# A two-layer mixture block on one Trainium2 core: the experts' gate and up products with all eight K-tiles in three reduced-precision passes

## The reference

```python
D_MODEL = 1024; SEQ = 512; DEPTH = 2
N_GROUPS = 4; EXPERTS_PER_GROUP = 4; N_EXPERTS = 16; TOP_E = 2; EXPERT_FF = 256

def hier_moe(h, w_rg, b_rg, w_re, b_re, w_g, w_u, w_d):
    g_logits = (h @ w_rg + b_rg)                       # one of 4 groups for each token
    _, g_sel = lax.top_k(g_logits, 1)
    ...
    e_val, e_sel = lax.top_k(e_in_group, TOP_E)        # two of its 4 experts
    weights = jax.nn.softmax(e_val, axis=-1) * p_group
    gate = jnp.sum(one_hot(expert_id, N_EXPERTS) * weights[..., None], axis=2)
    hid = jax.nn.silu(jnp.einsum('bsd,edf->bsef', h, w_g)) * jnp.einsum('bsd,edf->bsef', h, w_u)
    hid = hid * gate[..., None]
    return jnp.einsum('bsef,efd->bsd', hid, w_d)
```

## Time and profile before

| what | value |
|---|---|
| median of three runs | 1389.27 us (1387.7 to 1389.38) |
| the profiled execution's own time | 1387.39 us |
| its span | 1385.6 us |
| PE busy | 1351.8 us, 98% |
| DVE, ACT, POOL busy | 892.1, 580.0, 761.6 us |
| expert loops | about 519 to 684 us and 1202 to 1373 us |

### The profile page before, as it was taken

How to read it: one execution, slowest core, us unless ns; L and a number is a source line. 1 busy time by engine, 2 the same in 40 slices (tenths; PEclk the granted TensorE clock), 3 DMA queues, 4 the chain that set the end, 5 groups by cost and what they waited for, 6 DMA issues and landing times.

```text
span 1385.6 us, 19946 instructions
## 1 busy us (share of the span) xinstructions
PE 1351.8 (98%) x6972; PEld 1046.3 (76%) x6972; DVE 892.1 (64%) x2057; ACT 580.0 (42%) x1238; POOL 761.6 (55%) x603
## 2 busy tenths in 40 slices
PE   7999999999999999999789999999999999999997
PEld 5788877777777876777577888777777778677774
DVE  4487866646684347988446787665566741588882
ACT  4323334343433135676343432434334321466761
POOL 4566654454345664567555576455444457546673
PEclk9999999999999999999989999999999999999999
DMA  5436422223222569999632242222223128699993
GB/s 155 131 93 175 128 71 87 62 78 105 84 67 67 203 269 349 354 371 369 135 116 76 61 137 78 79 77 72 83 90 90 62 76 291 238 368 365 357 345 87
DMA packets 115066, 225.35 MB, mean 163 GB/s; under 512 B 18666, under 2 KB 28324, under 8 KB 114958
## 3 DMA queue, kind: packets, MB, share of 16 engines
q1 hardware_dynamic: 102526, 198.64, 42.6%
q0 software_dynamic: 9936, 16.81, 5.3%
q10 hardware_dynamic: 2496, 8.52, 1.6%
HBM read 216.52 MB, written 31.25 MB: 179 GB/s over the span
## 4 chain that ended last, share of the span: by engine, by line
PE 92%; DVE 4%; POOL 1%; issue 1%; ACT 1%; DMA 1%; POOLq 0%; SPq 0%; DVEq 0%; ACTq 0%
PE bank L987 23%; PE bank L989 22%; PE bank L988 22%; PE bank L1284 5%; PE bank L1163 4%; PE bank L1175 3%; PE bank L1196 2%; PE bank L1244 2%; PE bank L1116 1%; PE bank L1186 1%; POOL w_lo L842 1%; PE bank L1129 1%; DVE probs L2003 1%; DVE mixed L1820 1%; PE bank L1254 1%
## 5 line engine op out<-in xcount | busy, mean ns | idle before, releaser
L836 POOL TENSOR_SCALAR w_hi<-raw 128x1024 fp32r<-128x1024 f32 (+2 forms) x142 | 149.8, 1055 | 409.3 <-PE bank L989 406.6
L842 POOL TENSOR_TENSOR w_lo<-raw,w_hi 128x512 fp32r<-128x512 f32 (+2 forms) x288 | 359.4, 1269 | 16.4 <-ACT w_hi L1732 4.6
L988 PE MATMUL bank<-w_hi,hT_lo 128*128 128x512 f32 (+2 forms) x696 | 258.7, 372 | 0.0
L987 PE MATMUL bank<-w_lo,hT_hi 128*128 128x512 f32 (+2 forms) x576 | 216.8, 376 | 2.0 <-DVE hT_lo L1828 1.0
L989 PE MATMUL bank<-w_hi,hT_hi 128*128 128x512 f32 (+2 forms) x576 | 211.7, 368 | 0.0
L987 PE MATMUL bank<-hT_lo,w_hi 128*128 128x512 f32 x384 | 159.4, 415 | 0.0
L989 PE MATMUL bank<-hT_hi,w_hi 128*128 128x512 f32 x384 | 150.7, 392 | 0.0
L988 PE MATMUL bank<-hT_hi,w_lo 128*128 128x512 f32 x384 | 150.2, 391 | 0.0
L988 PEld LDWEIGHTS bank<-w_hi,hT_lo 128*128 128x128 f32 x696 | 131.5, 189 | 20.2
L987 PEld LDWEIGHTS bank<-w_lo,hT_hi 128*128 128x128 f32 x576 | 108.7, 189 | 28.0 <-issue 8.5
L989 PEld LDWEIGHTS bank<-w_hi,hT_hi 128*128 128x128 f32 x576 | 108.6, 188 | 17.9
(11 more groups left out here) (359 smaller groups left out, 2836.5 us busy)
## 6 DMA issues: line engine op xcount, KB each, us to landing
raw<-in_w_gate SPq DMA_DIRECT2D x48, 512.0 KB, 3.8
work<-in_w_ff_gate SPq DMA_DIRECT2D x46, 512.0 KB, 6.5
work<-in_w_ff_up SPq DMA_DIRECT2D x46, 512.0 KB, 8.7
work<-in_w_ff_down SPq DMA_DIRECT2D x23, 1024.0 KB, 8.6
raw<-in_w_in SPq DMA_DIRECT2D x40, 512.0 KB, 3.6
raw<-in_w_branch SPq DMA_DIRECT2D x24, 512.0 KB, 3.6
w_lo_raw<-in_w_ff_down SPq DMA_DIRECT2D x10, 1024.0 KB, 8.1
X<-in_w_ff_gate SPq DMA_DIRECT2D x20, 512.0 KB, 5.8
```

The source lines that it names most:

```text
L836: nc.gpsimd.tensor_scalar(w_hi[:, two, :, 0:w], raw[:, slot, :, 0:w], 1.0, 0.0, ALU.mult, ALU.add).then_inc(split_hi, 1)
L842: last = nc.gpsimd.tensor_tensor(w_lo[:, two, kk, 0:w], raw[:, slot, kk, 0:w], w_hi[:, two, kk, 0:w].bitcast(F32), ALU.subtract)
L987: nc.tensor.matmul(out_ap, s_hi, m_lo, start=start, stop=False)
L988: nc.tensor.matmul(out_ap, s_lo, m_hi, start=False, stop=False)
```

## The change

`SPLIT_FROM` becomes 0: K-tiles 0 and 1 of experts 2 to 15 too are done in three passes. High and low parts of gate and up are made by whole pieces of four K-tiles (2048 elements a partition), two an expert, and the two pieces stand apart in the order of ACT and DVE. ACT takes over from DVE the right half of the rows (but expert 15's) and the hidden tile's high part. The overflow lists move from `e` 2 and 3 to 3 and 5, their product on PE from 5 to 7, and the wait for it from 6 to 8. The rest renames semaphores.

```diff
-FIRST_SPLIT, SPLIT_FROM = 2, 2
-SPLIT_PAIRS = (8 - SPLIT_FROM) // 2
+FIRST_SPLIT, SPLIT_FROM = 2, 0
...
-        gu_hi_bufs = [[oT_hi[:, 0:2], oT_hi[:, 2:4], oT_lo[:, 0:2], oT_lo[:, 2:4]],
-                      [hT_lo[:, 0:2], hT_lo[:, 2:4], hT_hi[:, 4:6], hT_hi[:, 6:8]]]
+        gu_hi_bufs = [[oT_hi[:, 0:4], oT_lo[:, 0:4]], [hT_lo[:, 0:4], hT_hi[:, 4:8]]]
...
-                    if e == 5:
+                    if e == 7:
                         pe.wait_ge(e_hot, 1)
...
-            def gate_up_hi(e):
-
-                for part, kk, kt in split_tiles():
-                    if kt == SPLIT_FROM or kk == 0:
-                        act.wait_ge(arrived(e, part), loaded(e, part))
-                    nc.scalar.activation(pair_hi_of(e, kt).rearrange("p k (h n) -> p k h n", h=2),
-                                         gate_up_piece(e, part)[:, :, kk:kk + 2, :].rearrange("p h k n -> p k h n"),
-                                         ACT.Copy).then_inc(gu_hi, 1)
+            def gate_up_hi(e, part):
+
+                first = 0 if part else SPLIT_FROM
+                act.wait_ge(arrived(e, part), loaded(e, part))
+                nc.scalar.activation(high_of(e, part), gate_up_piece(e, part)[:, :, first:4, :], ACT.Copy).then_inc(gu_hi, 1)
...
             def rows_down(e):
-                act.wait_ge(down_done, 2 * e + 1)
-                if e == 0:
-                    act.wait_ge(w_known, 1)
-                if e >= 4:
-                    act.wait_ge(y_out[l][e % 4], 16 * (e // 4))
-                nc.scalar.activation(xn[:, e % 4, 0:512], G[2][:, :], ACT.Copy,
-                                     scale=slot_weight[:, EXPERT_AT[e]:EXPERT_AT[e] + 1]).then_inc(y_act, 1)
-
+                for c in range(2 if e < N_EXPERTS - 1 else 1):
+                    act.wait_ge(down_done, 2 * e + c + 1)
+                    if e == 0 and c == 0:
+                        act.wait_ge(w_known, 1)
+                    if e >= 4 and c == 0:
+                        act.wait_ge(y_out[l][e % 4], 16 * (e // 4))
+                    nc.scalar.activation(xn[:, e % 4, c * 512:(c + 1) * 512], G[2 + c][:, :], ACT.Copy,
+                                         scale=slot_weight[:, EXPERT_AT[e]:EXPERT_AT[e] + 1]
+                                         ).then_inc((y_left, y_right)[c], 1)
+
+            def hidden_hi(e):
+                act.wait_ge(hid_turned, e + 1)
+                if e >= 2:
+                    act.wait_ge(down_done, 2 * (e - 1))
+                nc.scalar.activation(hid_hi[:, e % 2, :], T[e % 2][:, 0:FF], ACT.Copy).then_inc(hidT_hi, 1)
...
                     if e < N_EXPERTS - 1:
                         et_out(e + 1)
+                    if splits(e + 2):
+                        gate_up_hi(e + 2, 0)
+                    if 1 <= e < N_EXPERTS - 1:
+                        weights_hi(e)
                     if e >= 1:
                         rows_down(e - 1)
+                    if e < N_EXPERTS - 1:
+                        hidden_hi(e)
                     if e == N_EXPERTS - 1:
                         et_out(e + 1)
-                    if 1 <= e < N_EXPERTS - 1:
-                        weights_hi(e)
                     if splits(e + 2):
-                        gate_up_hi(e + 2)
+                        gate_up_hi(e + 2, 1)
...
+                    if splits(e + 1):
+                        gate_up_lo(e + 1, 1)
+                    if e == 0:
+                        hidden_lo(e)
+                        route_over()
+                    if splits(e + 2):
+                        gate_up_lo(e + 2, 0)
+                    if 1 <= e < N_EXPERTS - 1:
+                        down_lo_half(e)
...
+                    elif 1 <= e < N_EXPERTS:
+                        hidden_lo(e)
+                    if e == N_EXPERTS:
+                        rows_right(e - 1)
                     if e == 1:
                         route_rows()
-                    if splits(e + 2):
-                        gate_up_lo(e + 2)
-                    if e in (2, 3):
-                        route_blocks(e - 2)
-                    if e == 5:
+                    if e in (3, 5):
+                        route_blocks((3, 5).index(e))
+                    if e == 7:
```

More of the change, by code:

```diff
@@ L383, in first_native, with high_of @@
             return SPLIT_FROM if splits(e) else KT
-        def pair_hi_of(e, kt):
-            return gu_hi_bufs[e % 2][(kt - SPLIT_FROM) // 2]
+        def high_of(e, part):
+            first = 0 if part else SPLIT_FROM
+            return (gu_hi_bufs[e % 2][part].rearrange("p k n -> p (k n)")[:, 0:512 * (4 - first)]
+                    .rearrange("p (h k n) -> p h k n", h=2, n=FF))
         def tiles_of(slot_rows):
@@ L415, in in_runs @@
             return src.rearrange("a (j p k) n -> p (a j) (k n)", p=P, k=ROW_RUN)
-        def split_tiles():
-            return [(kt // 4, kt % 4, kt) for kt in range(SPLIT_FROM, KT, 2)]
         banks = [ctx.enter_context(nc.psum_tensor(f"bank{i}", [P, 512], F32)) for i in range(8)]
@@ L840, in split @@
                     if n == UNITS_K:
-                        pool.wait_ge(hi_by_act, kk + 1)
+                        pool.wait_ge(hi_by_left, kk + 1)
                     last = nc.gpsimd.tensor_tensor(w_lo[:, two, kk, 0:w], raw[:, slot, kk, 0:w],
@@ L903, in add_rows @@
                 def add_rows(e):
-                    pool.wait_ge(y_act, e + 1)
-                    pool.wait_ge(y_dve, e + 1)
+                    pool.wait_ge(y_left, e + 1)
+                    pool.wait_ge(y_right, e + 1)
                     if e == 0:
@@ L2271, in et_out, with gate_up_lo @@
                                         ALU.subtract).then_inc(et_dve, 1)
-            def gate_up_lo(e):
-                for n, (part, kk, kt) in enumerate(split_tiles()):
-                    v.wait_ge(gu_hi, split_pairs(e - 1) + n + 1)
-                    nc.vector.tensor_tensor(gate_up_low(e, part)[:, :, kk:kk + 2, :].rearrange("p h k n -> p k h n"),
-                                            gate_up_piece(e, part)[:, :, kk:kk + 2, :].rearrange("p h k n -> p k h n"),
-                                            pair_hi_of(e, kt).bitcast(F32).rearrange("p k (h n) -> p k h n", h=2),
-                                            ALU.subtract).then_inc(gu_lo, 1)
+            def gate_up_lo(e, part):
+                first = 0 if part else SPLIT_FROM
+                v.wait_ge(gu_hi, split_parts(e - 1) + part + 1)
+                nc.vector.tensor_tensor(gate_up_low(e, part)[:, :, first:4, :], gate_up_piece(e, part)[:, :, first:4, :],
+                                        high_of(e, part).bitcast(F32), ALU.subtract).then_inc(gu_lo, 1)
             def down_lo_half(e):
@@ L2286, in down_lo_half, with hidden_lo, rows_right @@
                                         w_hi[:, 1, :, :].bitcast(F32), ALU.subtract).then_inc(down_lo_dve, 1)
+            def hidden_lo(e):
+                v.wait_ge(hid_turned, e + 1)
+                v.wait_ge(hidT_hi, e + 1)
+                nc.vector.tensor_tensor(hid_lo[:, e % 2, :], T[e % 2][:, 0:FF], hid_hi[:, e % 2, :].bitcast(F32),
+                                        ALU.subtract).then_inc(hidT_done, 1)
+            def rows_right(e):
+                v.wait_ge(down_done, 2 * (e + 1))
+                if e >= 4:
+                    v.wait_ge(y_out[l][e % 4], 16 * (e // 4))
+                if e == 0:
+                    v.wait_ge(w_known, 1)
+                nc.vector.tensor_scalar(xn[:, e % 4, 512:1024], G[3][:, :], slot_weight[:, EXPERT_AT[e]:EXPERT_AT[e] + 1],
+                                        None, ALU.mult).then_inc(y_right, 1)
             def experts():
```

54 lines of the change are left out of this document (18 added, 36 removed).

## The result

| what | before | after |
|---|---|---|
| median beside each other | 1388.49 us (4 runs) | 1401.8 us (4 runs, 1401.23 to 1402.97) |
| ratio | | 1.0097, 95% interval 1.0082 to 1.0112 |
| profiled execution, its span | 1387.39, 1385.6 us | 1401.77, 1400.0 us |
| PE, DVE, ACT, POOL busy | 1351.8, 892.1, 580.0, 761.6 us | 1350.9, 927.0, 623.5, 811.9 us |

The kernel became 13.3 us slower. The direction is the forecast's (slower, at a chance of 0.53), the size is not: 5.5 us were forecast, and the result lies above the range's end of 1399.5.

The account below looks back on a forecast made before the run. PE, holding 92% of the span, was taken as the bound, with DVE, ACT and POOL close behind. -9.8 - 0.4 + 5.3 + 10.4 = +5.5 us on 1389.27 gave 1394.8 us, range 1384.5 to 1399.5.

Parts of the forecast that it names:

- PE's gain: Experts 2 to 15, both layers: 56 K-tiles in three passes instead of full float32 save 0.176 us each, -9.8 us.
- the tail: End of each layer: ScalarE takes the eviction before the last hidden tile's copy, 0.2 us a layer, -0.4 us.
- The entry: Start of the expert stage: PE waits 2.4 and 2.9 us before the weight counts, behind ACT's late hidden copy; +5.3 us.
- DVE's term: Experts: DVE's 7.4 us of work plus two 1.1 us handovers with POOL exceed PE's 9.38; 5.2 a layer, +10.4 us.
- it is a toss: After expert 7 DVE has caught up; one handover or two an expert is open, half counted, 0.8 us a layer.
- rival A: Experts: only one handover each, DVE needs 8.5 of 9.38 us; -2.9 us, 1386.4 us; chance 0.2.
- rival C: DVE is the bound in all experts, also after 7: 7.5 us a layer, +10.1, 1399.4 us; chance 0.1.
- 1.4 + 3.0: Per layer: DVE late by 0.23 us in each of experts 1 to 6, 1.4; overflow lists no longer absorbed, 3.0.
- The tie: Whether POOL asks before or after DVE's second piece begins; the walk had the two within 0.05 us.
- the held gather: POOL gather started 0.16 us after a DVE subtraction lasted 2.00 us; such holding could leave one handover.
- Rival B: One handover an expert, but late weight loads cost 1 to 1.5 us a layer: no change, 1389 us; chance 0.2.

Follow-up runs that it names:

- e8: e7 with a semaphore of its own for the second half of each expert's gate/up rows; 1378.95 us.
- e1: The changed kernel, but ACT copies expert 0's hidden high part ahead of expert 2's first high part instead of behind it; 1395.97 us.
- e2: The changed kernel, but DVE makes both halves of the down weights' low part from expert 1 on and POOL none; 1392.64 us.
- e14: The changed kernel with the edits of e1 and e8, POOL's two subtractions an expert kept; 1397.04 us.
- e13: e8, but POOL makes one 128x512 subtraction of the low down rows an expert, DVE the other and the right half; 1385.89 us.
- e7: The changed kernel with the edits of e1 and e2 together; 1382.34 us.
- e4: The changed kernel with the overflow lists back in experts 2 and 3 and PE's overflow counts two experts earlier; 1400.53 us.
- e5: The kernel before with all eight K-tiles in three passes, pairs and old order kept; 1398.75 us.
- e6: The changed kernel with two K-tiles left as before; new order, whole pieces, ACT's evictions and spread lists stay; 1394.25 us.
- e3: The changed kernel with POOL's subtraction for experts 1 to 14 left out and not replaced, so the output is not the block's; 1390.65 us.
- e12: e2 with three matmuls on ready data put before PE's weight counts in expert 1; 1387.91 us.

## Why the prediction was wrong in size

The forecast's sum, term by term, against the runs. They form a chain: before 1387.8, e8 1378.95, e1 1395.97, after 1401.8.

- **PE's gain**, -10.2 with the tail: e8, in which nothing else costs, is 8.8 us under before. Right to 1.4; most of the missing part is in the steps with the lists and their product (9.79 us in e8 where e2 has 9.42, 11.36 where e2 has 11.17, in each layer).
- **The entry**, +5.3: e1 gives back 5.8. The idle time itself was 4.98 (2.31 + 2.67), a little less than said; half clock for 3.4 us in the second layer was not foreseen. The forecast counted the wait and took the clock behind it for granted. That this did not show is luck: it fell in one layer only, and DVE's lateness took it up there (see e1). In e2, where DVE is not late, it fell in both and twice as long.
- **DVE**, +10.4: e1 minus e8 is 17.0 (e14 minus e8: 18.1). This is the step that failed: the size of DVE's term; it lacks 6.6 us, and the error of the whole forecast was 7.8 against the ratio of its own runs. The mechanism and its price were right: meetings of 1.10 us, two an expert, DVE's work 7.4, the order of it and PE's wait for `hidden_lo`. Three parts of its size were wrong, the third under the next point. First "after expert 7 ... it is a toss ... half, 0.8": it is no toss, the down weights meet POOL in every expert. A late DVE stays late, as the case against rival A had it, and I did not carry that sentence into the sum. Second, 9.61 us an expert was DVE's work without any wait: the turns last 9.64 and 9.80, on average 9.73, since DVE still waits 0.11 us for ACT in every other expert. So each late expert costs 0.35 us, not 0.23 or 0.115: 7 x 0.35 = 2.5 in place of 0.8 a layer (the steps of e1 behind expert 8 are together 2.4 longer than e8's). In experts 2 to 7 the steps of e1 are together 6.2 us longer than those of e8; the forecast had 1.4 + 3.0 there. Together 8.6 a layer, more than rival C's bound of 7.5, which was made of the same 9.61; of all the rivals C, at 0.1, came nearest.
- **What experts 2 to 7 lack in that sum** is for the most part a term that the forecast put at nothing without a reason: `route_rows`. It names the routing work of experts 1 to 6 but prices only the two lists. DVE's timeline of e1, from the end of expert 1's turn to expert 8's product:

```profile
548.68 0.41 DVE L2295 TENSOR_TENSOR hT_lo<-bank,hT_lo 128x256 fp32r<-128x256 f32 x1
549.02 0.16 DVE L2224 TENSOR_SCALAR raw<-rank 128x8 f32<-128x8 f32 x1
...
550.60 0.42 DVE L2318 TENSOR_TENSOR sq<-sq,bank 128x256 f32<-128x256 f32 x1
...
569.84 0.15 DVE L2249 SCALAR_TENSOR_TENSOR raw<-raw,rank 128x8 f32<-128x8 f32 x1
...
571.59 0.42 DVE L2318 TENSOR_TENSOR sq<-sq,bank 128x256 f32<-128x256 f32 x1
...
613.12 0.42 DVE L2318 TENSOR_TENSOR sq<-sq,bank 128x256 f32<-128x256 f32 x1 [1.30 <-ACT sq L1778]
```

  `route_rows` takes 1.58 us (549.02 to 550.60), the lists 1.75 (569.84 to 571.59) and 1.56, and DVE has no gap over 0.04 us until 611.8. The turns without routing work are 9.62 us, 0.25 over PE's 9.37 in e8. 6 x 0.25 + 1.58 + 1.75 + 1.56 = 6.4, near the 6.2 measured; e8 itself pays about 0.5 for the routing work there, so a few tenths stay open. In before and in e8 PE lost nothing behind `route_rows` (steps of 9.66 and 9.32 us from expert 2 to 3); in e1 that step is 10.20. This is an estimate from the timelines; no run takes `route_rows` away.
- **Rival A** (one handover) named the right lever. The tie in my walk never fell its way. Nor did the row of the held gather help it: the gathers of after last 1.03 us in the median and 1.27 at most, where the held one took 2.00. And its price was too low: e13, which has one by construction, a semaphore of its own for the second half, and no entry wait, is 1.9 us faster than before; with the entry's 5.8 that makes 3.9 slower, where A had 2.9 faster.
- **Rival B** (the stream) had no part in after: with PE held up by DVE no load was late. It came true as soon as DVE was relieved (e7), at 3.4 us, near the 2 to 3 that B had given it. And it was not the 377 GB/s: e8.
- The Trainium skill ("SBUF — State Buffer", Who interferes with whom) says that a DVE instruction with two SBUF inputs contends with a GpSimd instruction that reads SBUF, and calls the shared port pair an exclusive lock. The rows agree: 2.31 to 3.38 and 1.21 to 2.31, the whole length of POOL's piece, wherever DVE asks just behind its start. Expert 14's down half asks in the middle of one (POOL from 677.17, DVE from 678.41) and takes 1.95, longer by what was left of it.

The lists' spread (e4) and, apart from the entry, the new order of the engines' work (e5, e6) were no causes.

## What to carry to other kernels

When an engine is filled to within a few per cent of the bound, its sum of work is a lower limit for its pace, not the pace: add the waits for the engines that it now runs in step with, price every piece of work that its old idle time hid (here the 1.6 us of `route_rows`), and assume that a lateness, once there, keeps itself up. Where DVE and GpSimd both subtract from SBUF to SBUF, give GpSimd's piece to DVE if DVE has room for the work itself: 0.6 us of own work (a 512-element piece in e13) replaced a meeting of 1.1. And a semaphore shared by two loads makes the first one wait for the second; look at it as soon as the consumer asks early.

## What the runs showed of the hardware

- Behind 1.5 to 2.9 us of idle PE at the entry the granted clock fell to half, for 3.4 us (after in its second layer, e3 in its first, e4 and e6 in both) or 6.8 us (e2 in both, e3 in its second); in after's first layer, behind 2.31 us, it did not, though in e3's, behind 2.30 us, it did. e5 had it for 3.4 us in both layers, behind two waits of 1.0 us that stood 0.4 apart. With PE busy on spare matmuls over the same wait (e12) it stayed at full. Half clock doubles PE's time for the stretch, so 3.4 us at half cost 1.7 us where PE is the bound (e6), and nothing that lasts where DVE is (after's second layer). No run here says what decides whether it comes.
- The Trainium skill ("TensorE: Matmul & The Clock Gate", Part 1) has a gate with two levels, 1.2 and 2.4 GHz; the rows show no third: products are 0.43 or 0.23 us apart.
- DMA engines without any idle share (1.05 in the window) were no bound on bytes: at 375 GB/s in e7 and 376 in e8 the same stream was late in the one and, but for one wait of 1.2 us, in time in the other.
- POOL's scatter with addition took 2.39 us where it started beside a DVE subtraction in SBUF (634.04 in after), 1.57 us with none beside it (681.68).
